# First quarter of a state recurrence run in parts between attention units, with key and value pages requested in a new order

## What is computed

```
def odd_prompt(h, ...):                     # 256 prompt tokens
    u, q_nope, q_pe, ckv, kpe = odd_heads(...)
    oc = s5_scan(u)                         # s[t] = abar * s[t-1] + B u[t], complex; Re(C s) + D u; half-GLU
    od = mla_core(q_nope, q_pe, k_nope, kpe, v)   # causal softmax attention, 8 heads
    return concatenate(oc, od) @ w_out

def odd_sample(h, ...):                     # 8 sequences: the same, with the state and pages of the past
    c_all = pool_ckv[pages]                 # 8 pages of 128 tokens x 128 latents per sequence
    k_all = pool_kpe[pages]                 # the pages' rotary keys, 32 wide
```

## Time and profile before

| | us |
|---|---|
| median of 3 runs | 2358.01 |
| profiled execution | 2355.39 |
| its span | 2353.6 |

### The profile page before, as it was taken

One profiled execution on the slowest core, in us unless ns is written; L12 is line 12 of the kernel. 1 busy time (PEld: TensorE's weight loads), 2 busy tenths in 40 slices (PEclk: granted clock), 3 DMA queues, 4 the chain that ended last, 5 costly groups with the idle time before them and its releaser, 6 DMA issues.

```text
span 2353.6 us, 38589 instructions
## 1 busy us (share of the span) xinstructions
PE 2024.6 (86%) x14393; PEld 1494.9 (64%) x14393; DVE 1157.0 (49%) x3460; ACT 650.8 (28%) x984; POOL 998.6 (42%) x874
## 2 busy tenths in 40 slices
PE   9788999999997668888888379999999987777777
PEld 4554899999995323333367146999999974233232
DVE  2554699433333532667566344997233333333333
ACT  1332345545551001111134012454555520000000
POOL 0111479830005665666414302588500026666665
PEclk9899999999999888999997579999999998889998
DMA  6474344544558999999912234254455569999998
GB/s 233 182 273 125 135 135 160 161 162 162 164 167 277 348 365 358 364 353 346 359 40 75 81 110 152 74 165 157 162 164 168 162 208 337 364 349 354 369 358 324
DMA packets 179914, 529.91 MB, mean 225 GB/s; under 512 B 22066, under 2 KB 49234, under 8 KB 179474
## 3 DMA queue, kind: packets, MB, share of 16 engines
q0 software_dynamic: 87296, 310.68, 36.2%
q1 hardware_dynamic: 91282, 216.25, 27.6%
q10 hardware_dynamic: 1152, 0.52, 0.1%
HBM read 524.69 MB, written 2.69 MB: 224 GB/s over the span
## 4 chain that ended last, share of the span: by engine, by line
PE 62%; another core or an unknown queue 8%; POOL 8%; issue 7%; DVE 6%; SPq 4%; DMA 3%; ACT 2%; DVEq 0%; ACTq 0%; POOLq 0%
PE bank L956 10%; PE bank L958 10%; PE bank L957 10%; PE bank L775 7%; PE bank L1020 6%; POOL u_low L710 3%; PE bank L996 3%; POOL v_slot L719 3%; PE bank L1038 2%; PE bank L1098 2%; SPq L449 2%; SPq L450 2%; POOL v_slot_of_columns L719 1%; DMA v_slot<-in_peer_v,v_rows 1%
## 5 line engine op out<-in xcount | busy, mean ns | idle before, releaser
L719 POOL DMA_INDIRECT v_slot<-in_peer_v,v_rows x417 | 393.8, 944 | 713.5 <-PE bank L958 441.1
L956 PE MATMUL bank<-h_parts,u_high 128*128 128x288 f32 x2048 | 607.0, 296 | 6.3 <-POOL u_low L710 4.6
L957 PE MATMUL bank<-h_parts,u_high 128*128 128x288 f32 x2048 | 604.4, 295 | 0.0
L958 PE MATMUL bank<-h_parts,u_low 128*128 128x288 f32 x2048 | 602.8, 294 | 0.0
L956 PEld LDWEIGHTS bank<-h_parts,u_high 128*128 128x128 f32 x2048 | 384.1, 188 | 10.1 <-POOL u_low L710 8.1
L958 PEld LDWEIGHTS bank<-h_parts,u_low 128*128 128x128 f32 x2048 | 385.8, 188 | 0.0
L957 PEld LDWEIGHTS bank<-h_parts,u_high 128*128 128x128 f32 x2048 | 384.6, 188 | 0.0
L1597 ACT CAST u_high<-u_slot 128x1024 fp32r<-128x1024 f32 x256 | 269.3, 1052 | 398.1 <-PE bank L958 241.9
L710 POOL TENSOR_TENSOR u_low<-u_slot,u_high 128x1024 fp32r<-128x1024 f32 x120 | 320.1, 2678 | 92.9 <-ACT u_high L1597 92.9
L1020 PE MATMUL bank<-v_slot,weight_columns 128*32 128x512 f32 x1412 | 265.6, 670 | 54.5 <-DMA v_slot<-in_peer_v,v_rows 28.7
L2170 DVE TENSOR_TENSOR u_low<-u_slot,u_high 128x1024 fp32r<-128x1024 f32 x136 | 166.7, 1226 | 274.6 <-ACT u_high L1597 274.6
(11 more groups left out here) (402 smaller groups left out, 2442.5 us busy)
## 6 DMA issues: line engine op xcount, KB each, us to landing
u_slot<-in_peer_ut SPq DMA_DIRECT2D x256, 512.0 KB, 3.5
w_q<-in_peer_w_q SPq DMA_DIRECT2D x8, 2048.0 KB, 14.6
region<-in_cache_a_kt SPq DMA_DIRECT2D x8, 960.0 KB, 12.7
region<-in_cache_a_v SPq DMA_DIRECT2D x8, 960.0 KB, 12.9
v_slot<-in_peer_v,v_rows POOLq DMA_INDIRECT x417
region<-in_ev_w_in SPq DMA_DIRECT2D x3, 2048.0 KB, 15.5
region<-in_pool_kv POOLq DMA_DIRECT2D x40, 128.0 KB, 5.5
ckv_t_norm<-in_pool_ckv SPq DMA_DIRECT2D x64, 64.0 KB
```

The source lines that it names most:

```text
L719: pool.indirect_dma_start(out=VS[l][slot], out_offset=None, in_=v_rows, in_offset=bass.IndirectOffsetOnAxis(ap=IDX[:, at:at + 1], axis=0)) ...
L956: pe.matmul(bank, uh, HR[:, 0, c, :], start=(c == 0), stop=False)
L957: pe.matmul(bank, uh, HR[:, 1, c, :], start=False, stop=False)
L958: ins = pe.matmul(bank, ul, HR[:, 0, c, :], start=False, stop=(c == KC - 1))
```

## The change

Of the four quarters of the prompt's recurrence, the first is moved between the units of the prompt's attention on VectorE, in eight parts: after unit 1, 2 and 3 one third of `states_products`, after 4 and 5 half of the scan, after 6, 7 and 8 one third of `states_turn_back`. The scans now write back to `BU[g]`; `T12` is gone and `XR` lies elsewhere. Behind `latent_scores(0)` VectorE has quarter 1, then part of quarter 2 between the first outputs and the rest ahead of `latent_scores(1)`; quarter 3 follows it. TensorE does `states_out(1)` ahead of `latent_scores(1)`.

The pages of round 1 are asked for in another order. SP asks for the turned latents of sequence 4 right after `s5_bt_ready`, ahead of the stores of the latents, and for those of sequence 5 and the mask `TBLDN` after `ut_ready`, ahead of `qct_ready`; for those of 7, whole, right after the rotary keys of 4. GpSimd asks for the rotary keys and the turned latents of 6 ahead of the values of 4, and has no part of 7. ScalarE asks for the rotary keys of 5 and 7 in place of the latents of 5. The diff, cut to its core:

```diff
-        T12 = [[tile_at(f"s5_tmp{n}{k}", [4, PAIRS], heads.at + 1024 * n + 512 * k) for k in range(2)] for n in range(2)]
-        XR = [[tile_at(f"s5_turned{g}{k}", [4, PAIRS], (HT_AT if g % 2 else heads.at + 2048) + 1024 * (g // 2) + 512 * k) for k in range(2)] for g in range(4)]
+        XR = [[tile_at(f"s5_turned{g}{k}", [4, PAIRS], at + 512 * k) for k in range(2)]
+              for g, at in enumerate((HT_AT, heads.at, heads.at + 1024, HT_AT + 1024))]
         W_OUT1 = [tile_at(f"w_out1_{n}", [KC, 512], at) for n, at in enumerate((HB[1], heads.at))]
...
                 load(S0, I["state_c"], "tbls_then_odd_small_loaded")
                 load(W_UKT, I["mla_w_ukt"], "tbls_then_odd_small_loaded")
                 load(W_GLU, I["s5_w_glu"], "tbls_then_odd_small_loaded")
...
@@ -600,26 +602,25 @@
                 for b in (0, 1):
                     pages_of(sp, KPP0[DR * b:DR * b + DR], I["pool_kpe"], b, "latents_loaded0")

+                sp.wait_ge(sem("ut_ready"), 4)
+                load(TBLDN, I["tbldn"], "tbl0_then_tbldn_loaded")
+                pages_of(sp, CKPT[5], I["pool_ckv"][:, :, 0:P], 5, "latents_loaded1")
                 sp.wait_ge(sem("qct_ready"), 10)
                 for b in (0, 1):
                     pages_of(sp, CKPT[b], I["pool_ckv"][:, :, 0:P], b, "latents_loaded0")
-                load(TBLDN, I["tbldn"], "tbl0_then_tbldn_loaded")

                 sp.wait_ge(sem("qg_ready"), 1)
                 for b in (0, 1, 2):
...

                 sp.wait_ge(sem("sd_scores"), 1)
-                for b in (4, 5):
-                    pages_of(sp, KPP0[DR * (b - 4):DR * (b - 3)], I["pool_kpe"], b, "latents_loaded1")
+                pages_of(sp, KPP0[0:DR], I["pool_kpe"], 4, "latents_loaded1")
+                pages_of(sp, CKPT[7], I["pool_ckv"][:, :, 0:P], 7, "latents_loaded1")
                 pages_of(sp, CKPV[5], I["pool_ckv"][:, :, P:2 * P], 5, "values_loaded1")

                 sp.wait_ge(sem("pages_used"), 4)
-                pages_of(sp, CKPV[6], I["pool_ckv"][:, :, P:2 * P], 6, "values_loaded1")
-
-                pages_of(sp, CKPT[4], I["pool_ckv"][:, :, 0:P], 4, "latents_loaded1")
-                pages_of(sp, CKPT[7][:, 0:4], I["pool_ckv"][:, :, 0:P], 7, "latents_loaded1", 0, 4)
-                pages_of(sp, CKPV[7], I["pool_ckv"][:, :, P:2 * P], 7, "values_loaded1")
+                for b in (6, 7):
+                    pages_of(sp, CKPV[b], I["pool_ckv"][:, :, P:2 * P], b, "values_loaded1")
                 sp.wait_ge(sem("samples_ready"), 1)
                 sp.wait_ge(sem("quarter_ready"), 5)
                 sp.wait_ge(sem("sd_scores"), 2)
@@ -734,12 +735,9 @@

...
                 pages_of(pool, CKPV[3], I["pool_ckv"][:, :, P:2 * P], 3, "values_loaded_by_pool0")
-                for b in (6, 7):
-                    pages_of(pool, KPP0[DR * (b - 4):DR * (b - 3)], I["pool_kpe"], b, "latents_loaded_by_pool1")
+                pages_of(pool, KPP0[2 * DR:3 * DR], I["pool_kpe"], 6, "latents_loaded_by_pool1")
+                pages_of(pool, CKPT[6], I["pool_ckv"][:, :, 0:P], 6, "latents_loaded_by_pool1")
                 pages_of(pool, CKPV[4], I["pool_ckv"][:, :, P:2 * P], 4, "values_loaded_by_pool1")
-
-                pages_of(pool, CKPT[6], I["pool_ckv"][:, :, 0:P], 6, "latents_loaded_by_pool1")
-                pages_of(pool, CKPT[7][:, 4:8], I["pool_ckv"][:, :, 0:P], 7, "latents_loaded_by_pool1", 4, 4)
...
                 def latent_scores(r):
                     if r == 0:
                         pe.wait_ge(sem("qabs_ready"), 1)
-                    pe.wait_ge(sem(f"latents_loaded{r}"), 16 * (4 * PAGES + 4 * r))
-                    pe.wait_ge(sem(f"latents_loaded_by_pool{r}"), 16 * (4 * PAGES - 4 * r))
+                    pe.wait_ge(sem(f"latents_loaded{r}"), 16 * (4 + 2 * r) * PAGES)
+                    pe.wait_ge(sem(f"latents_loaded_by_pool{r}"), 16 * (4 - 2 * r) * PAGES)
...
                 latent_values(0)
                 states_out(0)
                 latent_out_turn(0)
+                states_out(1)
                 latent_scores(1)
-                states_out(1)
+                states_out(2)
                 latent_turn(1)
-                states_out(2)
                 latent_values(1)
                 states_out(3)
                 latent_out_turn(1)
...
                 latent_turn(0)
                 states_in(3)
                 act.wait_ge(sem("pages_loaded"), 16)
-                pages_of(act, CKPT[5], I["pool_ckv"][:, :, 0:P], 5, "latents_loaded1")
+                for b in (5, 7):
+                    pages_of(act, KPP0[DR * (b - 4):DR * (b - 3)], I["pool_kpe"], b, "latents_loaded1")
                 latent_exp(1)
                 latent_turn(1)
...
                         second(n - 2)
+                    if between:
+                        between(n)
...
                     re, im = BU[g][:, 0], BU[g][:, 1]
                     out = XR[g]
-                    step(dve.tensor_tensor(out[0], cos, re, ALU.mult))
-                    step(dve.tensor_tensor(out[1], cos, im, ALU.mult))
+                    if part == 0:
+                        dve.wait_ge(sem("bu_ready"), 8 * (g + 1) + 4 * (g // 2))
+                        step(dve.tensor_tensor(out[0], cos, re, ALU.mult))
+                        step(dve.tensor_tensor(out[1], cos, im, ALU.mult))
+                    elif part == 1:
+                        step(dve.tensor_tensor(im, sin, im, ALU.mult))
+                        step(dve.scalar_tensor_tensor(out=re, in0=sin, scalar=-1.0, in1=re, op0=ALU.mult, op1=ALU.mult))
+                    else:
+                        step(dve.tensor_tensor(out[0], out[0], im, ALU.add))
+                        step(dve.tensor_tensor(out[1], out[1], re, ALU.add))
...
+                def states_scan(g, k):
+                    for q in range(4):
+                        step(dve.tensor_tensor_scan(BU[g][:, k, q, :], par[14][:, 4 * g + q:4 * g + q + 1].broadcast_to([P, PAIRS]),
+                                                    XR[g][k][:, q, :], 0.0, ALU.mult, ALU.add))
                     settle()
-                    step(dve.tensor_tensor(out[0], out[0], im, ALU.add))
-                    step(dve.tensor_tensor(out[1], out[1], re, ALU.add))
...
+                    turn, now = turns_of(g), (XR[g][0], BU[g][:, 0])
+                    if part == 0:
+                        step(dve.tensor_tensor(XR[g][0], turn[0], BU[g][:, 0], ALU.mult))
+                        step(dve.scalar_tensor_tensor(out=XR[g][1], in0=turn[1], scalar=-1.0, in1=BU[g][:, 1], op0=ALU.mult, op1=ALU.mult))
+                    elif part == 1:
+                        step(dve.tensor_tensor(BU[g][:, 0], turn[1], BU[g][:, 0], ALU.mult))
+                        step(dve.tensor_tensor(BU[g][:, 1], turn[0], BU[g][:, 1], ALU.mult))
+                    else:
+                        step(dve.tensor_tensor(now[0], now[0], XR[g][1], ALU.add))
+                        step(dve.tensor_tensor(now[1], now[1], BU[g][:, 1], ALU.add))
...
+                    if part == 2:
+                        say("quarter_ready")
+                        for k in range(2):
+                            step(dve.tensor_copy(LASTP[:, k, 4 * g:4 * g + 4], now[k][:, :, PAIRS - 1]))
+                        settle()
+                        if g == 3:
...
+                def first_quarter(n):
+                    if 1 <= n < 4:
+                        states_products(0, n - 1)
+                    if 4 <= n < 6:
+                        states_scan(0, n - 4)
+                    if 6 <= n < 9:
+                        states_turn_back(0, n - 6)
+
+                dve.wait_ge(sem("ut_ready"), 4)
+                prompt_attention([(p, qt) for p in range(4) for qt in range(2)], "prompt1", S_D, tables1, O1, SCALE_D, first_quarter)
...
                 latent_scores(0)
-                states_products(0)
                 out_of_sample_states()
-                states_scan(0)
-                states_turn_back(0)
-                states_products(1)
-                states_scan(1)
+                quarter(1)
                 latent_out(0)
-                states_turn_back(1)
                 out_of_states(0)
                 latent_out_turned(0)
+                states_products(2, 0)
+                states_products(2, 1)
+                out_of_states(1)
+                states_products(2, 2)
+                for k in range(2):
+                    states_scan(2, k)
+                for part in range(3):
+                    states_turn_back(2, part)
                 latent_scores(1)
-                states_products(2)
-                states_scan(2)
-                out_of_states(1)
-                states_turn_back(2)
-                states_products(3)
-                states_scan(3)
+                states_products(3, 0)
+                states_products(3, 1)
+                states_products(3, 2)
+                for k in range(2):
+                    states_scan(3, k)
                 out_of_states(2)
```

(14 more changed lines are left out.)

34 lines of the change are left out of this document (7 added, 27 removed).

## The result

| | before | after |
|---|---|---|
| median, us | 2356.3 (4 runs) | 2330.7 (4 runs) |
| ratio, 95% interval | | 0.9892 (0.9860 to 0.9925) |
| profiled execution, its span | 2355.4, 2353.6 | 2334.8, 2333.1 |

Two later series of the changed kernel, each with its own runs of the kernel before, gave 0.9874 (0.9841 to 0.9906) and 0.9879 (0.9854 to 0.9904).

A forecast was written before the change was run, and what follows sets the result against it. The order of page requests was taken to bound layer 1's mixing, VectorE's recurrence behind it. The last output moves from 1379.28 to 1351.2, 28.1 us; profiled 2355.39 becomes 2327.3, plus 2.6 for the median: 2329.9, range 2321 to 2341.

The forecast's parts named there:

- Quarter 0 and the lock: In the prompt's attention: moved quarter ends the last unit 6.3 us later, GpSimd's sample states hold VectorE another 3.
- the rival "less": Attention covers none of quarter 0, GpSimd's hold costs 4 us, clock stays 0.50: 18.4 us gained, 2339.6; chance 0.19.
- The lock: In the attention, VectorE's two-input SBUF operations wait for GpSimd's instructions on the samples' states: 3 us, bounds 0 and 4.
- 0.9 of this goes where VectorE waited for the absorbed queries anyway: Behind the attention: of the last unit's 6.3 us delay, 0.9 falls into an existing VectorE wait, leaving 5.3.
- d: Delay of the end of latent_scores(0), 5.3 + 3 = 8.3 us, passed on to GpSimd's value requests and latent_values(0).
- TensorE behind it: After latent_scores(0): latent_values(0) 4.6 us, states_out(0) and the turn 7.7, then states_out(1) 4.1 at clock 1.00.
- the rival "more": GpSimd's hold on VectorE costs nothing (3 us), states_out(0) runs at clock 1.00 (3.1): 34.3 us gained, 2323.7; chance 0.17.
- Keys: Round 1's keys of the samples' attention land at 1322 us instead of 1340.9, by the new order of page requests.
- The cover of 4 us: Ahead of latent_scores(1): margin by which round 1's keys and TensorE's first banks come before VectorE wants them.
- The keys stay late: Pages not limited by issue, round 1's land at 1340.9: 11.6 us gained, 2346.4, chance 0.04; late values too, 2358, 0.03.
- Value pages: Round 1 of the samples' attention: its value pages leave SP by 1335 us and are wanted at 1341.
- Moved unchanged: After the last out_of_states: gate, output projection and second mixer shift with it and keep their durations.

The follow-up runs named there:

- e3: Changed kernel with the four recurrence steps of the samples' states left out on GpSimd; last output at 109.0 us, ratio 0.9853 to the kernel before.
- e7: Changed kernel with more dummy matmuls in TensorE's waits in the prompt's attention; last output at 108.6 us, ratio 0.9869 to the kernel before.
- e1: Kernel before with only the new order of page requests and the counts TensorE waits for; last output at 107.4 us, ratio 0.9869.
- e4: Changed kernel with quarter 0 put back behind latent_scores(0); last output at 104.8 us, ratio 0.9863 to the kernel before.
- e9: e4 with 24 of the GLU's 32 matmuls ahead of states_out(3) and dummy matmuls in five TensorE waits; last output 107.2 us, ratio 0.9873.

## Why the prediction was right

2329.9 was predicted and 2330.7 measured, 28.1 us off the profiled chain and 27.1 measured. That both lie within 1 us is luck in part. By the medians 25.6 us were gained; the median of the kernel before was 2358.0 for the prediction and 2356.3 with its fourth run. And in the chain errors cancel, as follows. By its own steps, counted from `q_gained` (1243.65 is taken off each predicted time):

- **Quarter 0 and the lock.** Attention later by 6.3 + 3 = 9.3; measured 36.27 - 27.39 = 8.9 (7.3 against the second profile of the kernel before). The 2.9 us that the text calls idle ahead of the first unit are not: VectorE works 2.0 of them (the window of the earlier trace rows starts at 1243.00, the first unit at 1245.89). So 12 us and not 10 spoke against the rival "less". The lock was taken at 3 (0 to 4); VectorE's operations grew by 1.9 (the scans by 0.5, three of the six turning operations by 0.3 each, small ones by the rest), and GpSimd's states by 3.0, behind which it had nothing to do. The Trainium skill ("SBUF — State Buffer", "Who interferes with whom") has a GpSimd read and a VectorE instruction with two SBUF inputs exclude each other. This trace agrees: 1.89 us for four scans where GpSimd computes, 1.37 where it doesn't and in e3, though three of the six turning operations took their usual 0.69.
- **`latent_scores(0)`: the step that failed.** "0.9 of this goes where VectorE waited for the absorbed queries anyway": that wait grew instead, to 2.12, and the next one to 3.40, since TensorE's clock fell after its waits in the attention. d is 10.9 (49.55 - 38.70), not 8.3. Before the clock fell, TensorE had waits of 1.11 and 2.29 us between short bursts. The text had put a clock on the outputs but none on this step; e7 shows 6 us on it, of which some 4 to 5 came with the quarter.
- **TensorE behind it.** The clock that was lost there came back two steps on: `states_out(0)` ran at 1.00 in 4.1 us, where the text took the slow one with the turn, 7.7. That half of the rival "more" came true. The text had a row in which the clock rose after 10 us of work without a gap; here it rose at 1318, after 3 us of `latent_values(0)` and a wait of 2.51 ahead of it, so the fast `states_out(1)` was right for a reason that the text didn't have. Output 1 stands at 74.3, predicted 75.2.
- **Keys.** Wanted at 83.5 (predicted 84.1), in TensorE's hands at 79.85 (predicted 78.4). The cover of 4 us was used up to less than 2, but it held. "The keys stay late" is refuted by e1: with the same pages and another order of issue they came 27 us sooner. What the Trainium skill ("DMA: Bandwidth & Descriptors", "Issuing engines are not separate DMA queues") calls usual, that the issue is small beside the transfer, is not so for these pages: GpSimd took 27.3 us for 24 requests, and 2.1 us after it began the last one, at 1331.64, TensorE had its keys.
- **Value pages.** "Leave SP by 1335 and are wanted at 1341" (91.4 and 97.4): they left at 95.1, TensorE was ready at 92.2 and waited 4.4 us. It cost little, as quarter 3 was ready only 0.4 us after `latent_values(1)`; but `states_out(3)` behind that wait ran at 0.50, and turning back to the last output took 11.45, not 10.0.
- **The sum of it.** The last output was due at 107.55 and came at 108.55. Output 1 was 0.9 ahead of the forecast (a late `latent_scores(0)`, a fast `states_out(0)`), 0.5 of it was left where quarter 3 is turned back, and the slow `states_out(3)` cost 1.45.
- **After it.** "Moved unchanged" was 4.2 us too little, and the execution began the stage 10.2 later than the profile before. The predicted median stands on neither; they are part of what makes single runs differ.

The sum was right, and its account of who earns it was not. It entered the quarter's move as part of one gain. The runs put a price on each, at the last output: the requests alone earn 28.3 us, the quarter alone 3.5, both 27.1 (26.9, 2.1 and 25.7 against the second profile of the kernel before). With the pages on time the move costs 3.7 us against e4, the direct comparison (3.8 at the gate), and 1.2 against e1 (3.0 at the gate), which could be chance.

The way it costs can be followed. The move delays `latent_scores(0)` by 10.9 us: 8.9 in the attention and 2.0 behind it, at the lower clock; that this is just what a quarter takes is a coincidence. GpSimd's requests for the values of sequence 3 wait for its end, and `latent_values(0)` for them: it starts 11.8 us behind scores(0) in e4 and e7 and 12.0 in the changed kernel. Then come the two outputs, behind which VectorE has the rest of quarter 2. The keys were not what counted: e7 has them in TensorE's hands by 73.7, 6 us sooner than the changed kernel, and ends at the same time, its two outputs at the low clock. The idle 12.8 us of VectorE in the attention were no free room: of 10.9 + 1.9 us of work put in, 3.9 disappeared (5.5 against the second profile).

## What to carry to other kernels

Idle time of an engine is room only if nothing behind it issues the transfers that the next stage waits for: ask first which signal ends the stretch and who waits for it. The wait that is to be filled is itself the nearest room: in e4 quarter 2 fits into it with quarter 0 left where it was. Where two edits come together, price each alone and the two together, as the one may be paid for by the other. Count from an event at the stage's start when single executions differ by more ahead of it than the edit is worth.

## What the runs showed of the hardware

- A clock of 1.00 won at one place was lost at the next: e3 and e7 had it for `latent_scores(0)` (6 us sooner) and not for the outputs (7 us in place of 4.2, twice), the changed kernel the other way round, and all three end within 0.5 us. With work in the waits of the whole stage (e9) it stood at 1.00 from 1300 to 1336.
- In e9 TensorE was busy 6.00 of 6.00 us in both stretches from 1288 to 1300, and the clock still fell, to a mean of 0.87 and 0.56. It was at 1.00 up to 1292; from 1289.7 on TensorE ran the matmuls of `states_in`, with 32 rows, and it was back at 1.00 by 1300, after 5 us of dummies with 128 rows. What pulled it down wasn't tried. The Trainium skill ("TensorE: Matmul & The Clock Gate", "Why this matters for your kernels") tells the writer to avoid idle gaps between bursts of matmuls; these rows show a fall without one, as far as a profile can tell in which the ends of matmuls are modelled.
- From gate to end, 3.5 to 5 us less with the new requests on two chips, in single profiles, unexplained.
